# Large expert items fetched by full rows of gate and up, their chunks accumulated in seven PSUM banks

## The reference

```
tok = h.reshape(256, 1024)
top_v, top_i = lax.top_k(tok @ router, 2);  w = softmax(top_v)
gates = sum(one_hot(top_i, 8) * w, axis=1)
for e in range(8):
    out += gates[:, e:e+1] * ((silu(tok @ w_gate[e]) * (tok @ w_up[e])) @ w_down[e])
```

## Time and profile before

| | |
|---|---|
| median of 3 runs | 1270.13 us (1268.98 to 1270.4) |
| the profiled execution | 1269.83 us, its span 1268.1 us |
| PE busy in the span | 1234.1 us (97%) |
| DVE, ACT busy | 637.3 us (50%), 565.2 us (45%) |
| weights and other data | 424.48 MB, mean 335 GB/s |

### The profile page before, as it was taken

One profiled execution on the slowest core, in us unless ns is written; L12 is line 12 of the kernel. 1 busy time (PEld: TensorE's weight loads), 2 busy tenths in 40 slices (PEclk: granted clock), 3 DMA queues, 4 the chain that ended last, 5 costly groups with the idle time before them and its releaser, 6 DMA issues.

```text
span 1268.1 us, 18552 instructions
## 1 busy us (share of the span) xinstructions
PE 1234.1 (97%) x7266; PEld 875.2 (69%) x7266; DVE 637.3 (50%) x755; ACT 565.2 (45%) x871; POOL 99.5 (8%) x260
## 2 busy tenths in 40 slices
PE   9998999999999999999999999999999999999787
PEld 8988999999989944588853468884347887332232
DVE  6887765555765501488831168880226886010001
ACT  6665554443655511477730167770036775010001
POOL 1000000000000183100002100000310000110000
PEclk9999999999999999999999999999998999999999
DMA  9943544348533399999999999999999999999997
GB/s 329 373 139 129 199 173 173 122 166 264 194 117 117 134 425 428 403 412 416 428 423 426 421 407 415 416 426 423 428 407 412 415 424 384 423 429 423 426 429 293
DMA packets 89032, 424.48 MB, mean 335 GB/s; under 512 B 5457, under 2 KB 24050, under 8 KB 71282
## 3 DMA queue, kind: packets, MB, share of 16 engines
q1 hardware_dynamic: 88592, 422.76, 83.4%
q10 hardware_dynamic: 354, 0.54, 0.1%
HBM read 422.23 MB, written 1.05 MB: 334 GB/s over the span
## 4 chain that ended last, share of the span: by engine, by line
PE 87%; DMA 8%; DVE 2%; ACT 1%; SPq 1%; issue 1%; ACTq 0%; POOLq 0%; POOL 0%; DVEq 0%
PE psA L2067 9%; PE psY L2082 7%; PE psA L1694 7%; PE psB L2067 7%; PE psA L1696 7%; PE psA L1695 7%; PE psB L1694 7%; PE psB L1696 7%; PE psB L1695 7%; PE psY L1696 5%; PE psY L1695 5%; PE psY L1694 5%; DMA ring<-in_moe_w_gate 3%; DMA ring<-in_moe_w_up 2%; DMA ring<-in_moe_w_down 2%; PE psY L2035 1%
## 5 line engine op out<-in xcount | busy, mean ns | idle before, releaser
L1560 DVE TENSOR_TENSOR wlo<-ring,whi 128x2048 fp32r<-128x2048 f32 (+1 forms) x138 | 287.7, 2104 | 88.3 <-ACT whi L938 86.0
L938 ACT CAST whi<-ring 128x1024 fp32r<-128x1024 f32 x252 | 260.4, 1052 | 100.8 <-issue 34.6
L1307 DVE TENSOR_TENSOR wlo<-ring,whi 128x1024 fp32r<-128x1024 f32 (+2 forms) x104 | 152.3, 1484 | 19.4 <-ACT whi L754 19.3
L2067 PE MATMUL psA<-ring,resT 128*64 128x512 f32 x620 | 148.8, 597 | 13.2 <-DMA ring<-in_moe_w_gate 6.7
L754 ACT CAST whi<-ring 128x1024 fp32r<-128x1024 f32 (+1 forms) x134 | 133.4, 1023 | 60.4 <-PE psY L1696 28.2
L1625 DVE TENSOR_TENSOR rowbuf<-psY,rowbuf 128x512 f32<-128x512 f32 x28 | 18.6, 688 | 211.9 <-PE psY L2035 211.9
L2067 PE MATMUL psB<-ring,resT 128*64 128x512 f32 (+1 forms) x624 | 113.9, 486 | 0.0
L1694 PE MATMUL psA<-xhi,whi 128*128 128x256 f32 x368 | 105.0, 285 | 2.6 <-DVE wlo L1307 1.2
L1694 PE MATMUL psB<-xhi,whi 128*128 128x256 f32 x368 | 106.4, 289 | 0.0
L2067 PEld LDWEIGHTS psB<-ring,resT 128*64 128x64 f32 x624 | 44.9, 137 | 89.0 <-issue 89.0
L1695 PE MATMUL psA<-xlo,whi 128*128 128x256 f32 x368 | 102.8, 279 | 0.0
(11 more groups left out here) (364 smaller groups left out, 2148.3 us busy)
## 6 DMA issues: line engine op xcount, KB each, us to landing
ring<-in_moe_w_down SPq DMA_DIRECT2D x50, 2048.0 KB, 19.9
ring<-in_moe_w_gate SPq DMA_DIRECT2D x35, 1792.0 KB, 10.8
ring<-in_moe_w_up SPq DMA_DIRECT2D x32, 1792.0 KB, 17.7
ring<-in_moe_w_gate SPq DMA_DIRECT2D x18, 2048.0 KB, 20.1
ring<-in_moe_w_up SPq DMA_DIRECT2D x18, 2048.0 KB, 21.4
ring<-in_ffn_w_gate SPq DMA_DIRECT2D x5, 2048.0 KB, 7.8
ring<-in_ffn_w_up SPq DMA_DIRECT2D x5, 2048.0 KB, 8.0
ring<-in_ffn_w_down SPq DMA_DIRECT2D x5, 2048.0 KB, 7.9
```

The lines of the kernel that those rows point to most:

```text
L938: nc.scalar.copy(hi_of(NG + m, 2), item_part(ring, j, g, 2)).then_inc(hi_done, 2)
L1307: nc.vector.tensor_tensor(part_of(wlo, s, g, size), part_of(ring, s, g, size), f(hi_of(m, size)), ALU.subtract).then_inc(lo_done, size)
L1560: nc.vector.tensor_tensor(item_part(wlo, j, g, step), item_part(ring, j, g, step), f(hi_of(NG + m, step)), ALU.subtract).then_inc(lo_done, ...
L2067: ins = mm(few_bank(b)[half * FEW:(half + 1) * FEW, to:to + end - x], few_in[:, k, :], raw[:, x - q * W:end - q * W], start=k == 0, stop=k ...
```

## The change

Large items take the slots of the small ones: gate k = 0 to 7, up k = 0 to 7, each of seven cells (14 KB rows), then down 0 to 6. Slot 0 comes in three transfers of 2, 2 and 3 cells, slot 1 on in one (two where the ring wraps). All seven chunks of gate accumulate at once in seven banks (`big_bank`), then all seven of up in the same banks; the Silu results wait in `big_act`. The down sums move from psY to psA. The pieces of the split no longer all have 2 or 4 cells: they end at slots, at the ring's slots of eight and at the twelve of `whi`. `item_split(i + 1, 0, NE)` and `item_halve(i + 1, 0, NE)` split seven cells ahead of a large item, not eight. The banks of small items are taken in another order. The core of the diff:

```
+    item_slots = [(kind, k) for kind in ("gate", "up") for k in range(KD)] + [("down", d) for d in range(NE)]
+    item_cells = [NE if kind != "down" else GS for kind, at in item_slots]
+    FIRST_PARTS = [[2, 2, 3]]
+    def split_pieces(first_size, size):
...
+                n = min(first_size if j < len(FIRST_PARTS) else size, end - m, HL - (NG + m) % HL, GS - (BIG_FROM + m) % GS)
...
+    HI_PIECES, LO_PIECES = split_pieces(2, 2), split_pieces(2, 4)
...
+        def big_bank(c):
+            return (psA[:, 0, :], psA[:, 1, :], psB[:, 0, :], psB[:, 1, :], psY[:, 1, :], psY[:, 2, :], psY[:, 0, :])[c]
...
@@ ScalarE, large item @@
+                for k in range(KD - 1):
+                    done = item_split(i, done, item_from[k + 1] + AHEAD + 2)
+                for c in range(NE):
+                    act.wait_ge(group_used, used_at(i, item_from[KD - 1] + c + 1))
+                    nc.scalar.activation(in_blocks(big_act(c)), by_block(big_bank(c)), ACT.Silu).then_inc(m_silu, 1)
+                    done = item_split(i, done, item_from[KD - 1] + c + 1 + AHEAD + 2)
+                for k in range(KD - 1):
+                    done = item_split(i, done, item_from[KD + k + 1] + AHEAD + 2)
+                done = item_split(i, done, 2 * CELLS + 4)
+                hidden_hi(i, 0)
+                done = item_split(i, done, 2 * CELLS + GS)
+                hidden_hi(i, 1)
+                for d in range(NE):
+                    done = item_split(i, done, 2 * CELLS + GS * (d + 1) + AHEAD + 2)
+                    if d + 2 < NE:
+                        hidden_hi(i, d + 2)
@@ VectorE, large item @@
-                for j in range(IS):
-                    stop = min(GS * (j + 1) + AHEAD, IG)
-                    item_halve(i, done, stop, 4 if j else 2)
-                    done = stop
-                    for c in TURN_AFTER.get(j, []):
-                        hidden_lo(i, c)
...
+                for j in range(2 * KD - 1):
+                    done = item_halve(i, done, item_from[j + 1] + AHEAD)
+                multiply(i, 0)
+                multiply(i, 1)
+                done = item_halve(i, done, 2 * CELLS + 4)
+                hidden_lo(i, 0)
+                hidden_lo(i, 1)
+                done = item_halve(i, done, 2 * CELLS + GS)
+                multiply(i, 2)
+                done = item_halve(i, done, 2 * CELLS + GS + 4)
+                multiply(i, 3)
+                for d in range(NE):
+                    if d + 2 < NE:
+                        hidden_lo(i, d + 2)
+                    done = item_halve(i, done, 2 * CELLS + GS * (d + 1) + AHEAD)
+                    if d + 4 < NE:
+                        multiply(i, d + 4)
@@ TensorE @@
+                    if kind == "up" and k == 0:
+                        pe.wait_ge(m_silu, i * NE + (c + 1))
...
+                    if kind == "up" and k == KD - 1 and 3 <= c < 5:
+                        hidden_turn(i, c - 3)
...
+            def big_down(i, j, c):
+                pe.wait_ge(m_hlo, hlo_at(i, max(c, 1)))
...
+                for j, (kind, at) in enumerate(item_slots):
+                    if kind != "down":
+                        big_columns(i, j, kind, at)
+                        continue
+                    big_down(i, j, at)
+                    if at + 2 < NE:
+                        hidden_turn(i, at + 2)
```

More of the change, by code:

```diff
@@ L127, in lo_piece @@
         return 1 if m < single else 4 if m in ffn_groups and slots[group_of[m][0]][1] == GS else 2
[L130 to L137, removed]
+    IS = 3 * NE
     AHEAD_SLOTS = 2
@@ L159, in trunk @@
+    item_slot = {key: j for j, key in enumerate(item_slots)}
+    FS = len(item_slots)
+    item_cells = [NE if kind != "down" else GS for kind, at in item_slots]
+    item_from = [sum(item_cells[:j]) for j in range(FS)]
+    assert sum(item_cells) == IG and BANK_SUM[-1] == NE
     assert len(DOWN_ROWS) == NE and all(len(rows) == FBW for rows in DOWN_ROWS)
     MAX_ITEMS = E + 5
-    END_GATHER = [few_slot["down", 1], few_slot["down", 2]]
-    NEXT_SMALL_AT = few_slot["down", 6]
-    SUM_AT = {few_slot["up", 7]: (0, 1), few_slot["down", 3]: (1, 1), few_slot["down", 4]: (0, 0), few_slot["down", 5]: (1, 0)}
@@ L164, in trunk @@
[L164 to L170, removed]
+    END_GATHER = [item_slot["down", 1], item_slot["down", 2]]
@@ L171, in trunk @@
+    NEXT_SMALL_AT = item_slot["down", 6]
+    SUM_AT = {item_slot["up", 7]: (0, 1), item_slot["down", 3]: (1, 1), item_slot["down", 4]: (0, 0), item_slot["down", 5]: (1, 0)}
+    BIG_GATHER = item_from[item_slot["down", NE - 2]]
+    SPREAD_AT = item_slot["up", 6]
+    SCATTER_AT = [item_slot[at] for at in (("gate", 7), ("up", 1), ("up", 5), ("up", 6))]
     CELLS = GS * RING
     AHEAD_CELLS = GS * AHEAD_SLOTS
+    BIG_FROM = GS * ((NS + SHIFT) % RING)
+    FIRST_PARTS = [[2, 2, 3]]
+    def split_pieces(first_size, size):
+        pieces, m = [], 0
+        for j in range(FS):
+            end = item_from[j] + item_cells[j]
+            while m < end:
+                n = min(first_size if j < len(FIRST_PARTS) else size, end - m, HL - (NG + m) % HL, GS - (BIG_FROM + m) % GS)
+                pieces.append((m, n))
+                m += n
+        return pieces
@@ L174, in trunk, with first_part @@
+    HI_PIECES, LO_PIECES = split_pieces(2, 2), split_pieces(2, 4)
+    LO_AT = dict(LO_PIECES)
+    def first_part(j, m):
+        return [a for a, n in enumerate(FIRST_PARTS[j]) for q in range(n)][m - item_from[j]]
     assert LAST == E - 1 and FEW_AT[0] == 0 and len(FEW_AT) == 5
@@ L474, in part_of, with item_part @@
             return slot[:, g * GROUP:(g + size) * GROUP].rearrange("p (g n) -> p g n", n=GROUP)
[L476 to L480, removed]
+        def item_part(t, m, size):
+            at = (BIG_FROM + m) % CELLS
+            slot, cell = t[at // GS], at % GS
+            if m >= item_from[FS - 1]:
+                half, k = divmod(m - item_from[FS - 1], FBW)
+                return slot[:, :].rearrange("p (k h n) -> p h k n", h=2, n=GROUP)[:, half, k:k + size, :]
+            return slot[:, cell * W:(cell + size) * W].rearrange("p (g n) -> p g n", n=W)
         def hi_of(m, size):
@@ L507, in few_runs @@
             runs = []
-            for q in range(few_cells[j]):
-                x = few_from[j] + q
+            for q in range(item_cells[j]):
+                x = item_from[j] + q
                 if isinstance(i, int) and i == 0 and CELLS <= x < CELLS + AHEAD_CELLS:
@@ L527, in transfers @@
         def transfers(i, j):
-            kind, at = few_slots[j]
+            kind, at = item_slots[j]
+            if not few(i):
+                return len(few_runs(i, j)) if j >= len(FIRST_PARTS) else 1
             if kind != "down":
@@ L666, in big_item @@
             def big_item(i, e):
-                for j, (kind, c, wide, part) in enumerate(item_slots):
+                for j, (kind, at) in enumerate(item_slots):
+                    sp.reg_add(used_past, used_past, item_cells[j])
+                    sp.wait_ge(group_used, used_past)
                     if kind == "down":
[L669 to L684, removed]
@@ L928, in _, with item_split @@
             nc.scalar.copy(count[:, 1, :], before[:, :]).then_inc(count_set, 1)
[L930 to L938, removed]
+            def item_split(i, done, last):
+                while done < len(HI_PIECES) and HI_PIECES[done][0] < last:
+                    m, size = HI_PIECES[done]
+                    j = max(a for a in range(FS) if item_from[a] <= m)
+                    if j < len(FIRST_PARTS) and first_part(j, m + size - 1) < len(FIRST_PARTS[j]) - 1:
+                        for a in range(first_part(j, m), first_part(j, m + size - 1) + 1):
+                            act.wait_ge(first_full[j][a], 16 * (BIG_AT.index(i) + 1))
+                    else:
+                        act.wait_ge(item_full[j], landed_at(i, j))
+                    act.wait_ge(group_used, hi_free(i, m, size))
+                    nc.scalar.copy(hi_of(NG + m, size), item_part(ring, m, size)).then_inc(hi_done, size)
+                    done += 1
+                return done
             def gather_hi(i, q):
@@ L1006, in result @@
                 for half, part in enumerate(parts):
-                    nc.scalar.copy(part, psY[:, 0 if few(i) else half, :]).then_inc(y_out, 2 // len(parts))
+                    nc.scalar.copy(part, psY[:, 0, :] if few(i) else psA[:, half, :]).then_inc(y_out, 2 // len(parts))
             def few_rows(i):
@@ L1035, in expert @@
             def expert(i):
-                done = AHEAD
-                for j in range(IS):
-                    stop = min(GS * (j + 1) + AHEAD + 2, IG)
-                    item_split(i, done, stop)
-                    done = max(done, stop)
-                    for c in TURN_AFTER.get(j, []):
[L1042 to L1046, removed]
-                            nc.scalar.activation(in_blocks(hid_of(d)), by_block(psA[:, half_of(d), :]), ACT.Silu).then_inc(m_silu, 1)
```

(19 more changed lines are left out.)

159 lines of the change are left out of this document (74 added, 85 removed).

## The result

The changed kernel takes 1347.14 us (median of 5 runs, 1345.24 to 1347.41) against 1269.13 us (5 runs) for the kernel before: a ratio of 1.0608, interval 1.0593 to 1.0623. It is 6% slower. The forecast was 1350.

A forecast was written before the change was run, and what follows sets the result against it. PE and the DMA queue were nearly even, with PE the bound up to item 5's end. 1269.83 + 56.7 (64.8 less 8.1) + 23 for the clock = 1349.5, said as 1350; forecast 1334 to 1360 (0.47), range 1320 to 1366.

The forecast's parts named there:

- Down, the deciding term: Large items, down: split queued behind hidden_lo stalls PE 3.9 us before slots 2 to 5 (15.7), plus 1.1 for d = 0.
- Changeovers and start: Large items: PE stalls of 1.0 us at the start, 1.4 from gate to up, 2.4 from up to down.
- up to down: Large item's changeover: 0.7 us for a multiply behind a DVE piece, 1.7 for hidden_hi(1) behind two casts; 2.4 together.
- Gate to up: Large item's changeover: banks reused at once, ACT loses 3.6 us of its lead; stall 1.9, taken as 1.4 us.
- The idle time in all: Three large items on PE: each grows from 121.4 to 143.0 us, adding 3 x 21.6 = 64.8 us.
- The clock: Behind twelve idle stretches in large items: eight falls to half clock at 2.9 us each, 23 us; bounds 0 and 35.
- The sentence on twelve falls and 1361: Large items: by the Trainium skill's default throttled state all twelve stretches would drop the clock, time near 1361 us.
- The fetch: Gate and up of large items: 14 KB rows save 3.3 us an item, 9.9 for three, not to be had.
- Rival C: Whole kernel: fetch decides if DVE splits slot d + 1 before waiting for turn d + 2; 1260 to 1265.5 us; chance 0.05.
- Rival A: Large items: PE stalls but the clock stays or falls a few times; 1320 to 1334 us; chance 0.27.
- rival B: Large items: all clock falls happen, and more at the two changeovers; 1360 to 1372 us; chance 0.15.
- D: Whole kernel: the ring's room and item 7's 14 us soak up a part; 1295 to 1320 us; chance 0.05.

The follow-up runs named there:

- the swap: Changed kernel with only VectorE's order in down changed: halve to the end of slot d+1 first, hidden_lo(d+2) behind it; 1274.09 us, ratio 1.0041.
- mended: The swapped kernel with multiplies 0 and 1 before the halving of cells 112 to 115 and hidden_hi(1) directly behind hidden_hi(0); 1267.26 us, ratio 0.9989.
- The fill experiment: Changed kernel plus 15 extra matmuls of 512 columns behind the turn after down slots 1 to 4 of large items; 1323.08 us, ratio 1.0428.
- the runs without the third pass: The swapped kernel and the kernel before, each without the third pass of each cell in large items; 1258.53 us (14 KB rows) and 1268.00 us (old rows).
- the short rows: The swapped kernel with gate and up of large items, from slot 1 on, in transfers of at most two cells; 1274.15 us against 1274.09.
- the bad order in item 1 alone: The changed kernel's VectorE order in item 1 only, items 3 and 5 swapped; 1298.21 us, ratio 1.0224.

## Why the prediction was right, point by point

The time (1350 for 1347.14), its mechanism and its place were right. That it is out by 3 us only is in part luck: the idle time was forecast 10 us too long, and the clock and the base together 6 us too short. By terms:

- **Down, the deciding term.** Forecast 3.9 us before down slots 2 to 5 and 1.1 before the second half of slot 1. Measured 3.69 three times an item and 3.65 once (the longest in the waits above; the fourth is booked as "issue" on L2030, a gather that PE does first) and 0.80. Shown by the swap, which exchanged two steps and removed them all.
- **Changeovers and start.** Forecast 1.0 + 1.4 + 2.4 = 4.8 an item; in the swapped kernel all waits of PE together are 3.7 + 3.1 + 2.1 = 8.9 us for three items, 3.0 each. The mechanism named for up to down was right (0.7 for the multiply, 1.25 for the second `hidden_hi`, forecast 0.7 and 1.7, and both went when mended). Gate to up was priced at 1.4 and is some 0.3: ACT's loss of lead was argued from sums, while the waits show that the split was ahead by more than that.
- **The idle time in all.** Forecast 3 x 21.6 = 64.8 us; PE was idle for 18.0 + 18.5 + 18.3 = 54.8.
- **The clock.** Forecast eight falls of twelve at 2.9 us, 23 us. All twelve fell, at less each: PE was busy for 131.15 + 131.57 + 130.63 = 393.4 us where the swapped kernel needs 367.2, so 26.1 us, 2.2 a fall. The fill experiment gives 24.1 by another way. The number of falls and the price of one were both wrong, in opposite directions. The sentence on twelve falls and 1361 had the number right and the price of 2.9 wrong.
- **The base.** A large item needs PE for 122.4 us in the new order, not 121.4: 3 us more in three items, which no term had.
- **Sum.** Item 5 ends at 1150.9, forecast 1074.4 + 56.7 + 23 = 1154.1. From there the rest was called unchanged, and is, within 1.0 us.
- **The fetch.** 3.3 us an item, and "not to be had": both right, shown by the runs without the third pass and by the short rows. One reading beside it was wrong: SP issues as many transfers as before, 81 for the three large items, not fewer. No term rested on it.

**Where it failed.** Rival C was priced with a room of 22.1 us, the 14.0 us for which PE waits in item 7 and the 8.1 of the two starts; with the split keeping up it was to end between 1260 and 1265.5. The swapped kernel is that case, and it takes 1274. The 14.0 us are no room for anything that happens before the end of item 5. The ring is as full there as PE lets it be, with at most 56 cells on board, and the other 290 or so must still be fetched: 194 us to the end of the span in every kernel here that PE holds up; the waits in item 7 are a part of these 194. The prediction used this rule for its own sum, and forgot it two paragraphs on and in its opening, where it called the room some 14 us. A large item may grow by 8.1 / 3 = 2.7 us before the end moves, not by 7.4. The swapped kernel needs 376.2 us for its three items against 372.3 before, and its end is later by just that (and 0.5 of a later start).

Rival A (the clock stays) falls with the windows at 0.50. Of rival B the first half came true, all twelve fell; its time did not, because a fall cost 2.2 us and the changeovers brought none. D (a part soaked up) falls with the bad order in item 1 alone.

## What to carry to other kernels

In an in-order queue, look for each wait on another engine and ask what independent work stands behind it: here a step of 0.69 us, put one line too early, took away the lead of an engine that had nothing to do for a third of each large item. When work is reordered, check for each consumer which producer's step stands directly before the one that it needs, at the index where the loop really is (slot d + 1, not d + 2). And a wait for data seen at the end of a run is room only for delays that come after the buffer was last full: compare the time from that point to the end across kernels before counting it as slack.

## What was not expected of the hardware

The stretches at half clock behind equal waits of 3.69 us were of two lengths, 3.4 and 6.8 us (five of 6.8 and seven of 3.4), and none of the twelve waits went without one. Waits of 1.3 us and less never brought one in the swapped kernel, nor did the one of 2.04 in the kernel before. Extra matmuls whose results nobody reads made a kernel 24 us faster.
